# Five layer openings taken as a pair of weight pieces, rounded tokens first, and finer waits for attention outputs

## The chip, the core and the metric

The kernel runs on one core of a Trainium2 chip. The time is what the device needs for one launch, in microseconds (us). The inputs lie in HBM, all work is done by this core's engines: TensorE (PE) multiplies and transposes, its weight loads are listed as PEld; VectorE (DVE), ScalarE (ACT) and GpSimd (POOL) do the rest; SyncE (SP) issues nearly all loads of weights.

## The reference

A stack of layers on 256 tokens of width 1024, float32, cut here to what matters:

```python
# layer 0: sliding-window attention and a state-space mixer; layer 1: stick-breaking attention
hn = rmsnorm(x, norm); mixed = mixer(hn) @ w_out; x = x + mixed
hn = rmsnorm(x, ffn_norm[layer])
x = x + (silu(hn @ w_gate) * (hn @ w_up)) @ w_down          # d_ff 2816
# second block
x = x + mixer(rmsnorm(x, g_mix))    # gated linear attention and block attention, gated by sigmoid(z), then w_out
x = x + memory_attention(rmsnorm(x, g_cross), mem_n)        # w_cq, w_ckv, w_co
x = x + hier_moe(rmsnorm(x, g_moe)) # 32 experts of 512, two for each token
return rmsnorm(x, g_final)
```

## The kernel before

Weights come in **pieces** of 1 MB (128 x 2048 floats), in the order of the table `STREAM`. SP loads piece k into slab k % 6 of a ring once TensorE has freed that slab (`load`, L441, waits for the count `piece_used`). Products keep float32 accuracy by splitting both operands in a rounded part (`hi`) and the rest (`lo`): ScalarE rounds a piece into one of four slabs `piece_hi` (`piece_hi_part`, L765), VectorE subtracts it from the piece, in place (`piece_lo_part`, L1934, count `split`), and TensorE makes three products for each tile (`three_passes`, L1282): hi x hi, hi x lo, lo x hi (the trace shows them as L1285, L1286, L1287).

PSUM has eight banks. Banks 0 to 3 go round for **tiles**: tile n of the list `TILE_PLAN` has bank n % 4, and `open_tile` (L389) waits until tile n - 4 was emptied by VectorE or ScalarE. Banks 4 to 7 hold the 256 x 1024 product that ends a layer: two token blocks (`tb`) by two halves.

A layer opens so. The last output product is done piece by piece (`output_part_split`, L1235); VectorE adds its four banks to the residual X one after the other (`add_residual`, L1869). `output_done` (L1274) waits until the product is finished and frees its last piece. `norm` (L1145) turns X in 16 transposes into four tiles, one for two k-tiles each; the scale by the root is applied later (`keep_roots`, L1840, which reads what `spread_roots`, L1169, puts in bank 4). ScalarE writes the rounded tokens `HT_hi` of each tile (L755, count `ht_hi`), VectorE the rest `HT_lo` (L1922) and so empties the tile. The first piece of the layer (`feature_major_split`, L1296, or `gate_up` in `glu`, L1330) waits before each pair of k-tiles until `HT_lo` of that pair exists:

```python
                            if after and i == first and f == kt % 2 == 0:
                                wait_emptied(pe, after, kt // 2)
                            c = slice(f * P, (f + 1) * P)
                            ins = three_passes(b[:, f * T:(f + 1) * T], (wh[:, kt, c], wl[:, kt, c]),
                                               (hi[:, kt, :], lo[:, kt, :]), kt == 0, kt == KT - 1)
```

A piece of 256 output columns is 2 halves x 8 k-tiles x 3 = 48 products. `glu` does 11 units of a gate piece, an up piece and a down piece. Its unit 0 uses banks 0 and 1; it begins the ffn of both layers (norms 1 and 3). odd_q0 follows norm 2, g_q and g_k norm 4, c_q norm 6.

Attention outputs (two tiles `_o`) are rounded by ScalarE into `MT_hi` (L736) and their rest is taken by VectorE (L1863) before the next product reads them; TensorE waits for both tiles (`wait_all_emptied`, L404). In the mixer of the second block the order on TensorE is: the values of moba (`weighted_values`, L1392), the wait for moba_o, transposes of the gated output (g_oT, L1613), the wait for g_oT, pieces z 6 and z 7, then proj_g and proj_m.

The experts follow the router. Eight teams of four experts use 24 pieces each, without a split. SP may load the first 22 of them early, each when its slab is no longer needed (`put`, L494).

## Time and profile before

| | |
|---|---|
| time, median of 3 runs | 1400.45 us (1399.97 to 1400.62) |
| the profiled execution | 1398.65 us, of which span 1396.5 us |
| busy: TensorE, its weight loads | 1186.7 us (85%), 928.5 us (66%) |
| busy: VectorE, ScalarE, GpSimd | 676.8 us (48%), 469.3 us (34%), 27.0 us (2%) |
| mean granted clock of TensorE | 0.934 |
| read from HBM | 339.80 MB, 245 GB/s over the span |

Span is from the first to the last instruction in the trace; the time has some 2 us around it. In the forty slices of the page TensorE is busy at 0.9 from the fifth slice to the 27th, save one at 0.6 where the small steps of the gated linear attention are, and at 0.5 to 0.7 in the last thirteen. The transfers stand at 0.9 in those, at 0.3 to 0.6 before. An idle time in brackets stands ahead of the instruction whose row it is on, with what ended it.

### The profile page before, as it was taken

To read this page: it belongs to the slowest core of one execution; us is meant where nothing else is said; L and a number is where in the kernel's file an instruction comes from. 1 tells how busy PE (TensorE), PEld (TensorE's weight loads), DVE (VectorE), ACT (ScalarE), POOL (GpSimd) and SP (SyncE) were. 2 spreads that over 40 slices of the span, in tenths; PEclk is the share of its full clock that TensorE was granted. 3 is DMA by queue.
4 is the path that set the end of the run, shared out by engine and by line. 5 is a ranking of instruction groups with operands and counts; after the bars stand their busy time and mean duration, and the time that the engine had idled before them with its cause. 6 is when DMAs were issued, how large, how long until landed. Compare 5 with 4: busy or idle time off the path is not lost.

```text
span 1396.5 us, 19896 instructions
## 1 busy us (share of the span) xinstructions
PE 1186.7 (85%) x8160; PEld 928.5 (66%) x8160; DVE 676.8 (48%) x960; ACT 469.3 (34%) x599; POOL 27.0 (2%) x82
## 2 busy tenths in 40 slices
PE   6999999999999999999998999999674666756665
PEld 5886999998987999998896888884221221212121
DVE  7997475556778575556344857552110110101012
ACT  5555343334665443334344534441010100101001
POOL 2310000000000000000000000000000000000000
PEclk9989999999999999999996999999888988888788
DMA  9523365555434365556452345797999999999995
GB/s 255 120 57 121 107 220 190 189 187 180 144 120 144 112 221 191 188 184 208 139 176 66 121 151 181 314 367 325 421 421 422 422 422 421 422 422 421 423 420 220
DMA packets 137016, 343.41 MB, mean 246 GB/s; under 512 B 9818, under 2 KB 99036, under 8 KB 112372
## 3 DMA queue, kind: packets, MB, share of 16 engines
q1 hardware_dynamic: 135292, 337.96, 64.7%
q0 software_dynamic: 1552, 4.47, 1.8%
q8 instruction: 50, 0.82, 0.2%
q14 instruction: 18, 0.15, 0.0%
q10 hardware_dynamic: 104, 0.02, 0.0%
HBM read 339.80 MB, written 2.62 MB: 245 GB/s over the span
## 4 chain that ended last, share of the span: by engine, by line
PE 60%; DMA 23%; DVE 10%; ACT 3%; issue 3%; SPq 2%; POOL 0%; DVEq 0%; ACTq 0%; POOLq 0%
PE ps L1285 16%; PE ps L1287 15%; PE ps L1286 15%; DMA ring<-in_w_exp_down_dram 11%; DMA ring<-in_w_exp_up_dram 11%; PE ps L1764 4%; PE ps L1739 3%; SPq L526 1%; DVE piece_lo L1939 1%; ACT piece_hi L774 1%; PE ps L1161 1%; DMA MT<-in_ssm_b_im_dram 1%; PE ps L1389 1%; PE ps L1539 1%; PE ps L1685 1%
## 5 line engine op out<-in xcount | busy, mean ns | idle before, releaser
L1285 PE MATMUL ps<-HT_hi,piece_hi 128*128 128x256 f32 x1088 | 311.2, 286 | 7.2 <-DVE HT_lo L1930 4.3
L1286 PE MATMUL ps<-HT_lo,piece_hi 128*128 128x256 f32 x1088 | 308.9, 284 | 0.0
L1287 PE MATMUL ps<-HT_hi,piece_lo 128*128 128x256 f32 x1088 | 308.8, 284 | 0.0
L1939 DVE TENSOR_TENSOR piece_lo<-ring,piece_hi 128x2048 fp32r<-128x2048 f32 x118 | 266.9, 2286 | 83.8 <-ACT piece_hi L774 83.2
L774 ACT ACTIVATE piece_hi<-ring 128x2048 fp32r<-128x2048 f32 x118 | 223.0, 1912 | 196.1 <-PE ps L1287 161.3
L1285 PEld LDWEIGHTS ps<-HT_hi,piece_hi 128*128 128x128 f32 x1088 | 209.8, 193 | 10.8 <-issue 7.8
L1739 PE MATMUL ps<-ring,arena 128*32 128x512 f32 x992 | 139.8, 716 | 87.6 <-DMA ring<-in_w_exp_up_dram 67.6
L1286 PEld LDWEIGHTS ps<-HT_lo,piece_hi 128*128 128x128 f32 x1088 | 209.9, 193 | 0.9
L1287 PEld LDWEIGHTS ps<-HT_hi,piece_lo 128*128 128x128 f32 x1088 | 209.8, 193 | 0.0
L1739 PEld LDWEIGHTS ps<-ring,arena 128*32 128x32 f32 x992 | 38.9, 128 | 182.0 <-issue 181.5
L1764 PE MATMUL ps<-ring,arena 128*32 128x512 f32 x464 | 78.9, 799 | 51.3 <-DMA ring<-in_w_exp_down_dram 51.3
L1764 PEld LDWEIGHTS ps<-ring,arena 128*32 128x32 f32 x464 | 21.2, 140 | 101.1 <-issue 101.1
L2608 DVE COPY arena<-ps 128x512 f32<-128x512 f32 x8 | 5.5, 692 | 143.1 <-PE ps L1764 143.1
L2606 DVE TENSOR_TENSOR arena<-arena,ps 128x512 f32<-128x512 f32 x8 | 5.5, 688 | 137.8 <-PE ps L1739 137.8
L1285 PE MATMUL ps<-piece_hi,HB_hi 128*128 128x512 f32 x176 | 69.7, 396 | 0.0
L1286 PE MATMUL ps<-piece_lo,HB_hi 128*128 128x512 f32 x176 | 69.6, 396 | 0.0
L1287 PE MATMUL ps<-piece_hi,HB_lo 128*128 128x512 f32 x176 | 69.6, 395 | 0.0
L1285 PE MATMUL ps<-piece_hi,HT_hi 128*128 128x256 f32 (+1 forms) x192 | 58.2, 303 | 1.2 <-PE ps L1287 1.2
L1286 PE MATMUL ps<-piece_lo,HT_hi 128*128 128x256 f32 (+1 forms) x192 | 57.7, 300 | 0.0
L1287 PE MATMUL ps<-piece_hi,HT_lo 128*128 128x256 f32 (+1 forms) x192 | 57.7, 300 | 0.0
L1116 ACT ACTIVATE arena<-ps 128x512 f32<-128x512 f32 x8 | 4.8, 597 | 155.8 <-PE ps L1753 155.8
L1960 DVE TENSOR_TENSOR arena<-ps,arena 128x512 f32<-128x512 f32 x22 | 15.2, 692 | 84.3 <-PE ps L1287 84.2
(449 smaller groups left out, 1737.6 us busy)
## 6 DMA issues: line engine op xcount, KB each, us to landing
ring<-in_w_exp_gate_dram SPq DMA_DIRECT2D x64, 1024.0 KB, 18.6
ring<-in_w_exp_up_dram SPq DMA_DIRECT2D x60, 1024.0 KB, 17.6
ring<-in_w_exp_down_dram SPq DMA_DIRECT2D x58, 1024.0 KB, 16.4
ring<-in_ffn_w_gate_dram SPq DMA_DIRECT2D x22, 1024.0 KB, 5.7
ring<-in_ffn_w_up_dram SPq DMA_DIRECT2D x22, 1024.0 KB, 5.4
ring<-in_ffn_w_down_dram SPq DMA_DIRECT2D x22, 1024.0 KB, 7.3
ring<-in_w_in_dram SPq DMA_DIRECT2D x20, 1024.0 KB, 5.4
ring<-in_odd_w_in_dram SPq DMA_DIRECT2D x12, 1024.0 KB, 5.2
```

What stands on the lines that cost most here:

```text
L526: sp.dma_start(dst, src).then_inc(expert_loaded[slot], 16)
L774: act.activation(piece_hi[:, h % HI_SLABS, :], ring[:, k % RING, :], ACT.Copy).then_inc(hi_made, 1)
L1161: ins = pe.transpose(banks[kt // 2][:, c:c + P], (X if raw else XN)[:, tb, kt * P:(kt + 1) * P], ident[:, :])
L1285: pe.matmul(out, sh, mh, start=start, stop=False, skip_group_check=True)
L1286: pe.matmul(out, sh, ml, start=False, stop=False, skip_group_check=True)
L1287: return pe.matmul(out, sl, mh, start=False, stop=stop, skip_group_check=True)
L1389: ins = pe.transpose(b[:, c * P:(c + 1) * P], S[:, h, src * P:(src + 1) * P], ident[:, :])
L1539: ins = pe.matmul(b[0:16, 0:T], alr_w[:, kt, :], part[:, kt, :].bitcast(F32), start=(part is HT_hi and kt == 0), stop=(part is HT_lo and k ...
L1739: ins = pe.matmul(ps[own, 2 + up, :], mGT[:, kt, own], w[e][:, k4, :], start=(kt == 0), stop=(kt == KT - 1))
L1764: ins = pe.matmul(ps[own, 4 + c, :], mHT[:, 2 * half + f, own], w[e][:, f, c * 512:(c + 1) * 512], start=(half == f == 0), stop=(half == f ...
L1939: ve.tensor_tensor(piece_lo[k % RING][:, :], ring[:, k % RING, :], piece_hi[:, h % HI_SLABS, :].bitcast(F32), ALU.subtract).then_inc(split, 1)
L1960: ve.tensor_tensor(by_token(G), by_token(gate), roots[1 + 2 * layer][1].unsqueeze(1).to_broadcast([P, 2, T]), ALU.mult).then_inc(gate_scal ...
```

## The change

Four things, all on TensorE's queue, except for the last line of the diff, by which VectorE reads the gate and up of unit 0 from banks 6 and 7.

- At five openings the first two pieces of the layer are taken together (`opening_pair`). Their first halves go to banks 6 and 7, which do not belong to the round of tiles. For each pair of k-tiles TensorE waits for the rounded tokens only, does the eight products with `HT_hi`, then waits for `HT_lo` and does the other four. The second halves follow as before. The first piece is freed after its second half.
- `output_done` moves from ahead of the norm's transposes to behind the first four of them (norms 1, 2, 3, 4 and 7).
- odd_out (its last two pieces) and c_out wait for one tile of the attention output at a time.
- In the mixer the wait for moba_o moves to ahead of proj_m, and z 6 and z 7 to ahead of the wait for g_oT.

```diff
@@ -74,6 +74,9 @@
 SPLIT_NORMS = (1, 2, 3, 4, 5, 6)
+PAIR_BANKS = {("odd_q0", 0): 6, ("odd_q0", 1): 7, ("g_q", 0): 6, ("g_k", 0): 7, ("c_q", 0): 6, ("c_q", 1): 7}
@@ -384,7 +387,7 @@
         def bank(name, i):
-            return ps[:, TILE_NO[(name, i)] % 4, :]
+            return ps[:, PAIR_BANKS.get((name, i), TILE_NO[(name, i)] % 4), :]
@@ -1142,7 +1145,7 @@
-            def norm(n, wait=True):
+            def norm(n, wait=True, closes=None):
@@ -1161,6 +1164,8 @@
                         ins.then_inc(bank_full, 1)
+                        if closes and kt == 1:
+                            output_done(closes)
                 for _ in range(fillers[1]):
@@ -1232,9 +1237,11 @@
-            def output_part_split(name, pieces, first, opening, closing, hi, lo, ready=None):
+            def output_part_split(name, pieces, first, opening, closing, hi, lo, ready=None, tiles=None):
                 for n, i in enumerate(pieces, first):
+                    if tiles is not None:
+                        wait_emptied(pe, tiles, n - first)
                     if ready is not None:
@@ -1293,6 +1300,39 @@
+            def opening_pair(n, outs, parts):
+                c = slice(0, P)
+                for i in range(4):
+                    pe.wait_ge(ht_hi, 4 * SPLIT_NORMS.index(n) + i + 1)
+                    for kt in (2 * i, 2 * i + 1):
+                        for out, (wh, wl) in zip(outs, parts):
+                            pe.matmul(out[:, 0:T], wh[:, kt, c], HT_hi[:, kt, :], start=kt == 0, stop=False,
+                                      skip_group_check=True)
+                            pe.matmul(out[:, 0:T], wl[:, kt, c], HT_hi[:, kt, :], start=False, stop=False,
+                                      skip_group_check=True)
+                    wait_emptied(pe, f"norm{n}", i)
+                    for kt in (2 * i, 2 * i + 1):
+                        for out, (wh, wl) in zip(outs, parts):
+                            pe.matmul(out[:, 0:T], wh[:, kt, c], HT_lo[:, kt, :], start=False, stop=kt == KT - 1,
+                                      skip_group_check=True)
+            def feature_major_pair(n, tiles):
+                parts = [split_piece(FIRST_PIECE[name] + i, KT) for name, i in tiles]
+                outs = [bank(name, i) for name, i in tiles]
+                opening_pair(n, outs, parts)
+                c = slice(P, 2 * P)
+                for j, (out, (wh, wl)) in enumerate(zip(outs, parts)):
+                    for kt in range(KT):
+                        ins = three_passes(out[:, T:2 * T], (wh[:, kt, c], wl[:, kt, c]),
+                                           (HT_hi[:, kt, :], HT_lo[:, kt, :]), kt == 0, kt == KT - 1)
+                        if j == 1 and kt == 0:
+                            ins.then_inc(piece_used, 1)
+                    ins.then_inc(bank_full, 1)
+                pe.wait_ge(bank_full, full_count(*tiles[1]))
+                pe.nop().then_inc(piece_used, 1)
             def feature_major_split(name, count, hi=HT_hi, lo=HT_lo, first=0, after=None):
@@ -1330,15 +1370,23 @@
-                def gate_up(buf, n, it=None, wait=None, after=None):
+                def first_gate_up():
+                    parts = [split_piece(FIRST_PIECE[name] + j, KT) for j in range(2)]
+                    opening_pair(1 + 2 * layer, [ps[:, 6 + j, :] for j in range(2)], parts)
+                    c = slice(P, 2 * P)
+                    for j, (hi, lo) in enumerate(parts):
+                        for kt in range(KT):
+                            ins = three_passes(ps[:, 6 + j, T:2 * T], (hi[:, kt, c], lo[:, kt, c]),
+                                               (HT_hi[:, kt, :], HT_lo[:, kt, :]), kt == 0, kt == KT - 1)
+                        ins.then_inc(gu_full if j else piece_used, 1)
+                def gate_up(buf, n, it=None, wait=None):
                     if wait is not None:
...
                             for kt in range(KT):
-                                if after and j == f == kt % 2 == 0:
-                                    wait_emptied(pe, after, kt // 2)
                                 c = slice(f * P, (f + 1) * P)
@@ -1359,7 +1407,7 @@
-                gate_up(0, 0, after=f"norm{1 + 2 * layer}")
+                first_gate_up()
                 spread_roots(1 + 2 * layer)
@@ -1370,8 +1418,6 @@
                 down((count - 1) % 2, 3 * count - 1, base + count, stop=True)
-                pe.wait_ge(mix_full, 4 * (RESIDUAL_NO[name] + 1))
-                pe.nop().then_inc(piece_used, 1)
@@ -1498,11 +1544,10 @@
             output_part_split("even_out_a", range(2), 0, 2, 1, MT_hi, even_lo_of)
-            output_done("even_out")
-            norm(1, wait=False)
+            norm(1, wait=False, closes="even_out")
             glu(0)
-            norm(2, wait=False)
-            feature_major_split("odd_q0", 2, after="norm2")
+            norm(2, wait=False, closes="ffn0")
+            feature_major_pair(2, (("odd_q0", 0), ("odd_q0", 1)))
             spread_roots(2)
@@ -1522,15 +1567,14 @@
                 weighted_values(name, A1, lambda h, kb: ov[:, kb, 512 * half + 64 * h:512 * half + 64 * h + 64])
-                wait_all_emptied(pe, name + "_o")
-            output_part_split("odd_out", range(2, 4), 2, 0, 3, MT_hi, odd_lo_of)
-            output_done("odd_out")
-            norm(3, wait=False)
+                if half == 0:
+                    wait_all_emptied(pe, name + "_o")
+            output_part_split("odd_out", range(2, 4), 2, 0, 3, MT_hi, odd_lo_of, tiles="sb1_o")
+            norm(3, wait=False, closes="odd_out")
             glu(1)
-            norm(4, wait=False)
-            feature_major_split("g_q", 1, after="norm4")
+            norm(4, wait=False, closes="ffn1")
+            feature_major_pair(4, (("g_q", 0), ("g_k", 0)))
             spread_roots(4)
-            feature_major_split("g_k", 1)
             token_major_split("g_v", 2)
@@ -1604,7 +1648,6 @@
             weighted_values("moba", PT2, lambda h, kb: m_v[:, kb, 64 * h:64 * h + 64])
-            wait_all_emptied(pe, "moba_o")
             pe.wait_ge(gla_out, 1)
@@ -1613,16 +1656,17 @@
                 ins.then_inc(bank_full, 1)
+            feature_major_split("z", 2, first=6)
             wait_all_emptied(pe, "g_oT")
-            feature_major_split("z", 2, first=6)
             projection_split("proj_g", MT_hi[:, 0:4, :], mixer_lo[:, 0:4, :])
+            wait_all_emptied(pe, "moba_o")
             projection_split("proj_m", MT_hi[:, 4:8, :], mixer_lo[:, 4:8, :])
...
             norm(6, wait=False)
-            feature_major_split("c_q", 2, after="norm6")
+            feature_major_pair(6, (("c_q", 0), ("c_q", 1)))
             for name in ("mem_k", "c_q"):
@@ -1650,10 +1694,8 @@
                 ins.then_inc(bank_full, 1)
-            wait_all_emptied(pe, "c_o")
-            output_part_split("c_out", range(2), 0, 0, 1, MT_hi, lambda kt: c_lo[:, kt, :])
-            output_done("c_out")
-            norm(7, wait=False)
+            output_part_split("c_out", range(2), 0, 0, 1, MT_hi, lambda kt: c_lo[:, kt, :], tiles="c_o")
+            norm(7, wait=False, closes="c_out")
             logits = [open_tile(pe, "router", tb)[:, 0:36] for tb in range(2)]
@@ -1954,7 +1996,8 @@
                     E, G, H = GE[:, buf, :], GH[:, buf, :], HB[:, buf, :]
-                    gate, up = ps[:, 2 * buf, :], ps[:, 2 * buf + 1, :]
+                    first_bank = 6 if u == 0 else 2 * buf
+                    gate, up = ps[:, first_bank, :], ps[:, first_bank + 1, :]
                     by_token = lambda v: v.rearrange("p (f t) -> p f t", t=T)
...
```

TensorE's queue, with the semaphores that a row waits for, at the opening of the first ffn: before, behind the last transposes (L1161).

```order
L1161 MATMUL ps<-ident,X 128x128 [waits residual_ready]
L1161 MATMUL ps<-ident,X 128x128 x5
L1285 MATMUL ps<-HT_hi,piece_hi 128x256 [waits vector_emptied,piece_split]
L1286 MATMUL ps<-HT_lo,piece_hi 128x256
L1287 MATMUL ps<-HT_hi,piece_lo_54 128x256
L1285 MATMUL ps<-HT_hi,piece_hi 128x256
L1286 MATMUL ps<-HT_lo,piece_hi 128x256
L1287 MATMUL ps<-HT_hi,piece_lo_54 128x256
L1285 MATMUL ps<-HT_hi,piece_hi 128x256 [waits vector_emptied]
L1286 MATMUL ps<-HT_lo,piece_hi 128x256
```

And with the change (the transposes are L1164; `piece_lo4_54` and `piece_lo5_55` are the fine parts of the two pieces):

```order
L1164 MATMUL ps<-ident,X 128x128 [waits residual_ready]
L1164 MATMUL ps<-ident,X 128x128 x5
L1310 MATMUL ps<-HT_hi_56,piece_hi_49 128x256 [waits tokens_hi_made,piece_split]
L1312 MATMUL ps<-HT_hi_56,piece_lo4_54 128x256
L1310 MATMUL ps<-HT_hi_56,piece_hi_49 128x256
L1312 MATMUL ps<-HT_hi_56,piece_lo5_55 128x256
L1310 MATMUL ps<-HT_hi_56,piece_hi_49 128x256
L1312 MATMUL ps<-HT_hi_56,piece_lo4_54 128x256
L1310 MATMUL ps<-HT_hi_56,piece_hi_49 128x256
L1312 MATMUL ps<-HT_hi_56,piece_lo5_55 128x256
L1317 MATMUL ps<-HT_lo_57,piece_hi_49 128x256 [waits vector_emptied]
L1317 MATMUL ps<-HT_lo_57,piece_hi_49 128x256 x3
```

The products with `HT_lo` stand behind all eight with `HT_hi`; the first row waits for the rounded tokens instead of the emptied tile.

The mixer, between the values of moba (L1400, L1401) and piece z 6 (L1285), before. Which count of `vector_emptied` a row waits for is not printed: for the first transpose it is the second tile of moba_o, for z 6 the second of g_oT.

```order
L1400 MATMUL ps<-arena 64x256 [waits scalar_emptied]
L1401 MATMUL ps<-arena 64x128
L1613 MATMUL ps<-ident,arena 128x128 [waits gla_out_ready,vector_emptied]
L1613 MATMUL ps<-ident,arena 128x128 x3
L1613 MATMUL ps<-ident,arena 128x128 [waits scalar_emptied]
L1613 MATMUL ps<-ident,arena 128x128 x3
L1285 MATMUL ps<-HT_hi,piece_hi 128x256 [waits piece_split,vector_emptied]
```

And with the change:

```order
L1446 MATMUL ps<-arena 64x256 [waits scalar_emptied]
L1447 MATMUL ps<-arena 64x128
L1656 MATMUL ps<-ident,arena 128x128 [waits vector_emptied,gla_out_ready]
L1656 MATMUL ps<-ident,arena 128x128 x3
L1656 MATMUL ps<-ident,arena 128x128 [waits scalar_emptied]
L1656 MATMUL ps<-ident,arena 128x128 x3
L1292 MATMUL ps<-HT_hi,piece_hi 128x256 [waits vector_emptied,piece_split]
L1293 MATMUL ps<-HT_lo,piece_hi 128x256
```

The rows are in the same order here; the first transpose now waits for a tile of probabilities (moba_pt) only, and z 6 (L1292) for the first tile of moba_o. The two pieces of z stand ahead of the wait for g_oT.

## Rows read from the trace of the kernel before

**Rows 1.** The page: the chain of work that ended last, shares of the span by engine.
```profile
PE 60%; DMA 23%; DVE 10%; ACT 3%; issue 3%; SPq 2%; POOL 0%; DVEq 0%; ACTq 0%; POOLq 0%
```

**Rows 2.** Waits of TensorE, summed: engine, line, waited for: us, times, longest.
```profile
PE ps L1739 <- DMA ring<-in_w_exp_up_dram: 67.6, 14, 6.3
PE ps L1285 <- DVE HT_lo L1930: 4.3, 5, 1.4
```

**Rows 3.** Busy time (PE, PEld, DVE, ACT, POOL) in a stretch, clock, DMA share, GB/s.
```profile
945.00:950.00 5.00, 4.15 (x38) 3.17 (x41) 2.08 (x9) 1.14 (x4) 0.00 (x0) 1.00 0.22 90
```

**Rows 4.** Timeline of TensorE at norm 1 and ffn0: start, us, instruction, idle before and releaser.
```profile
139.11 1.94 PE L1161 MATMUL ps<-ident,X 128*128 128x128 f32 x16 [0.41 <-DVE X L1879]
141.77 0.36 PE L1285 MATMUL ps<-HT_hi,piece_hi 128*128 128x256 f32 x1 [0.73 <-DVE HT_lo L1930]
...
144.85 0.28 PE L1285 MATMUL ps<-HT_hi,piece_hi 128*128 128x256 f32 x1
...
147.73 0.28 PE L1285 MATMUL ps<-HT_hi,piece_hi 128*128 128x256 f32 x1
```

**Rows 5.** Timeline of VectorE, then of ScalarE, there.
```profile
137.18 2.47 DVE L1879 TENSOR_TENSOR X<-X,ps 128x512 f32<-128x512 f32 x4
140.75 3.23 DVE L1930 SCALAR_TENSOR_TENSOR HT_lo<-ps,cols,HT_hi 128x256 fp32r<-128x256 f32 x8 [1.10 <-PE ps L1161]
...
139.77 3.03 ACT L761 ACTIVATE HT_hi<-ps,cols 128x256 fp32r<-128x256 f32 x8 [4.84 <-PE ps L1161]
...
155.86 1.90 ACT L774 ACTIVATE piece_hi<-ring 128x2048 fp32r<-128x2048 f32 x1
```

**Rows 6.** Timeline of VectorE, then of TensorE, behind norm 4.
```profile
655.42 0.42 DVE L1843 COPY arena<-ps 128x256 f32<-128x256 f32 x1
...
656.48 2.28 DVE L1939 TENSOR_TENSOR piece_lo<-ring,piece_hi 128x2048 fp32r<-128x2048 f32 x1
...
660.57 0.36 PE L1285 MATMUL ps<-piece_hi,HT_hi 128*128 128x256 f32 x1 [0.30 <-PE ps L1287]
```

**Rows 7.** Timeline of ScalarE, then of TensorE, at norm 6 and c_q.
```profile
884.65 3.03 ACT L761 ACTIVATE HT_hi<-ps,cols 128x256 fp32r<-128x256 f32 x8 [1.57 <-PE ps L1161]
...
886.62 0.36 PE L1285 MATMUL ps<-HT_hi,piece_hi 128*128 128x256 f32 x1 [1.36 <-DVE HT_lo L1930]
```

**Rows 8.** Around c_out: VectorE; TensorE; the stretch 920 to 925 us.
```profile
919.88 0.69 DVE L1867 TENSOR_TENSOR c_lo<-ps,MT_hi 128x512 fp32r<-128x512 f32 x1 [2.73 <-ACT MT_hi L739]
...
921.85 0.47 PE L1285 MATMUL ps<-piece_hi,MT_hi 128*128 128x512 f32 x1 [1.53 <-DVE c_lo L1867]
...
933.59 1.94 PE L1161 MATMUL ps<-ident,X 128*128 128x128 f32 x16 [0.41 <-PE ps L1287]
...
920.00:925.00 5.00, 3.47 (x16) 2.62 (x15) 3.46 (x3) 0.60 (x1) 0.85 (x4) 1.00 1.02 429
```

**Rows 9.** Timeline of VectorE, then of TensorE, at odd_out.
```profile
438.86 0.69 DVE L1867 TENSOR_TENSOR odd_lo<-ps,MT_hi 128x512 fp32r<-128x512 f32 x1 [1.98 <-ACT MT_hi L739]
...
440.95 0.47 PE L1285 MATMUL ps<-piece_hi,MT_hi 128*128 128x512 f32 x1 [1.53 <-DVE odd_lo L1867]
```

**Rows 10.** The mixer: VectorE; TensorE; the stretch 807 to 809 us.
```profile
802.59 1.31 DVE L1867 TENSOR_TENSOR mixer_lo<-ps,MT_hi 128x512 fp32r<-128x512 f32 x2 [0.45 <-ACT MT_hi L739]
...
798.14 1.53 PE L1389 MATMUL ps<-ident,arena 128*128 128x128 f32 x12 [1.64 <-DVE arena L1859]
...
804.00 1.06 PE L1613 MATMUL ps<-ident,arena 128*128 128x128 f32 x8 [1.53 <-DVE mixer_lo L1867]
806.75 0.55 PE L1285 MATMUL ps<-HT_hi,piece_hi 128*128 128x256 f32 x1 [1.69 <-DVE mixer_lo L1867]
...
812.44 0.41 PE L1287 MATMUL ps<-HT_hi,piece_lo 128*128 128x256 f32 x1
...
807.00:809.00 2.00, 2.00 (x10) 2.00 (x11) 2.00 (x2) 0.55 (x1) 0.00 (x0) 0.50 0.74 279
```

**Rows 11.** Timeline of TensorE: first product with expert weights.
```profile
948.92 3.64 PE L1739 MATMUL ps<-ring,arena 128*32 128x512 f32 x32 [0.61 <-ACT arena L1101]
```

## The prediction

> **What bounds the kernel now.** I read the profile from its end. The chain of work that ended last [rows 1] gives TensorE 60% and the transfers 23%: the program has two halves. The waits of TensorE, summed [rows 2], show the second half: in the experts it waits 67.6 us for up weights, so there the weight stream sets the pace. The same view shows the first half: apart from the experts, the largest sum is 4.3 us for the fine parts of the tokens (HT_lo), in five waits. TensorE is otherwise fed without a break, one 256-column product each 0.12 us. So in the first half only a wait of TensorE is time, and each of them is short.
>
> Whether time saved there reaches the end is answered by the busy time by stretch [rows 3]. Between 945 and 950 us the transfers are at 0.22 of full, moving 90 GB/s: the first team's slabs are loaded, and the rest of the stream waits until TensorE has used one. The stream starts from a signal of TensorE, and then runs without a gap, so a microsecond saved before it is a microsecond at the end.
>
> **Openings of a layer.** TensorE turns the tokens (16 transposes, from 139.11 us), then waits 0.73 us until the fine part of the first two k-tiles exists, and starts at 141.77 [rows 4]. The second half of that first piece starts at 144.85, so 24 products took 3.08 us where 24 x 0.12 is 2.88: 0.20 us more of small waits. ScalarE rounds from 139.77, eight in 3.03 us, VectorE takes the fine part from 140.75, eight in 3.23 us [rows 5]: a pair of k-tiles each 0.81 us, where TensorE eats one in 0.72. The rounded first pair is there at about 139.77 + 0.8 = 140.6, before the transposes end (about 141.04). The change begins with eight products on rounded tokens (0.96 us), then four on the fine ones (0.48 us): fine pair 0 is needed at 142.0 and there at 141.6, and a pair now lasts 1.44 us against 0.81. Both the wait and the small ones go: 0.73 + 0.20. Four openings are like this (odd_q0, the second ffn and g_q are the others): the five waits of [rows 2] are 4.3 us together, and the longest, of c_q, is 1.4, which leaves 0.73 for each. 4 x 0.93 = **3.7 us**.
>
> At 647 us g_q and g_k become a pair, and one drain between a group's last product and the next step goes, the 0.30 us at 660.57 [rows 6]: **0.3 us**. What is new there: the roots are spread after both pieces, 48 products or 5.8 us later. VectorE took them at 655.42 (after other work, so this is the latest date), and the fine part of g_v 1 (2.28 us) queues behind them and one tile of g_q. With the 0.9 won it takes the roots by 655.4 + 5.8 - 0.9 = 660.3 and ends with g_v 1 by 660.3 + 0.4 + 0.7 + 2.3 = 663.7. TensorE began g_v 0 at 660.57, now at 659.3, and wants g_v 1 5.8 us later, at 665.1. Covered by 1.4 us.
>
> At c_q the wait is longer, 1.36 us: ScalarE starts at 884.65, TensorE at 886.62 [rows 7]. With the change TensorE starts on the first rounded pair, at about 884.65 + 0.8 and some 0.15 for the signal, 885.6: 1.0 us, and 0.20 of small waits as above: **1.2 us**.
>
> The first piece of each pair frees its slot 24 products (2.9 us) later. Behind that: SP's next load into that slot, and ScalarE's rounding into that slab. ScalarE comes to the next slab only at 155.86 [rows 5], while the slot is now free at about 141.04 + 72 x 0.12 = 149.7, where it was free at 147.7. Cost 0. Were the cover gone, it would be up to 2 us at each of five places.
>
> **Own-product waits.** The wait for the last output product moves behind the first four transposes. The first row of [rows 4] has 0.41 us of idle there. But those of the second token block wait for VectorE's third addition, which ends about 139.05 (first addition 137.18, four in 2.47 us, [rows 5]). So at norm 1 only two transposes go ahead, 0.2 us; at norms 2 to 4 VectorE ends later and nothing is won; at norm 7 (933.59, [rows 8]) the additions keep up, and most of the 0.41 goes: 0.4. Together **0.6 us**.
>
> **Attention outputs.** At odd_out TensorE waits 1.53 us for both fine tiles and starts at 440.95; the first tile's part starts at 438.86 and takes 0.69 [rows 9]. It may now start at about 439.65: **1.3 us**. The second is needed a piece (24 x 0.23 = 5.6 us) later. At c_out the start is 921.85, the first tile's part is done at 919.88 + 0.69 [rows 8]: start 920.67, **1.2 us**.
>
> **The mixer.** Now: transposes of g_oT at 804.00 after 1.53 us of waiting for the fine parts of moba_o, then z 6 at 806.75 after 1.69 us more [rows 10]. With the change the transposes follow the values at about 804.00 - 1.53 = 802.5, take 8 x 0.12 us, and z 6 needs only tile moba_o 0, whose part starts at 802.59 and is done 0.65 us later. Start at about 803.4: **3.3 us**. Two pieces (11.5 us) then cover both conversions. Their weights were split before that in the kernel before, by queues that do not move.
>
> **The clock.** [...] The single gap of 1.53 us at c_out stands in a stretch with the clock at 1.00 (920 to 925, [rows 8]), so I take the low stretch as gone: **2.5 us**. The bounds are 0 and 2.5.
>
> **Sum.** 3.7 + 0.3 + 1.2 + 0.6 + 1.3 + 1.2 + 3.3 = 11.6, with the clock 14.1 us. The profiled execution took 1398.65 us, so it becomes 1384.6; the median of the runs is 1.8 us above it, 1400.45 - 14.1 = **1386 us**. A difference of 0.2% (2.8 us) is about what a measurement of this kernel tells from none.
>
> **The price that no row has** is that consecutive products now alternate between banks 6 and 7, 48 in each opening, 240 in all. Nearest row: the up piece, in the next bank, starts at 147.73 [rows 4], which is 144.85 + 24 x 0.12: the change of bank costs nothing. I take 0. The other end is the start-up of a stream: the product after 141.77 comes 0.20 us later, 0.08 more; 240 x 0.08 = 19 us. The lower end is 0 too, since the work on the array is the same.
>
> [...]
>
> **Rivals.**
> 1. *The gaps go, the low clock at 806 us stays* (or comes at another place; the stretch of small products before it is not changed, and the first gap of 1.64 us remains). Then 11.6 us: 1389. Chance 0.25.
> 2. *Part of it is taken over by other waits*: late slots, or the roots behind both pieces of g. Half of the gain: about 1394. For it: the rounding chain ScalarE, VectorE, TensorE is a queue of few slabs; against it: the slacks above. Chance 0.08.
> 3. *The stream hides it.* The 22 early pieces must be loaded between 883 and 945 us, and that window gets shorter by 1.2 + 1.2 + 0.4 = 2.8 us. If the stream were full throughout, nothing would be won: 1400. Against it: the share of 0.22 at 945 to 950 [rows 3], nearly 4 us of pause in these 5. Chance 0.03.
> 4. *Slower: alternating banks.* If each of the 240 products lost more than (11.6 + 2.8) / 240 = 0.060 us, the kernel would be slower by over 0.2%. [...] Chance 0.04. [...]
>
> **Chances.** Forecast 0.60; rivals 0.25, 0.08, 0.03, 0.04. Faster by over 0.2%: 0.93; within: 0.03; slower: 0.04. The range reaches from 1382, one more saving of the clock's size (other stretches of small products may keep the full clock too) and 0.2 us more at each of nine waits, to 1393, which takes in rival 1 and most of rival 2. That holds 0.9; the runs of one kernel differ by 0.6 us.
>
> **What would show it.** Waits for HT_lo: none left (one for HTm_lo, 1.4, stays). First product of an opening at once after the transposes. The products of an opening 0.12 us apart: if 0.2, rival 4. One wait of about 0.6 us or less at c_out and odd_out. z 6 about 1 us after the last of the moba values, and the clock at 1.00 there; if it is at 0.50, rival 1. The stretch from the first expert product (now at 948.92, [rows 11]) to the end of the span unchanged at 1396.5 - 948.9 = 447.6 us: if it is longer by what the first half won, rival 3. The forecast is wrong if TensorE shows a new wait for piece_lo in the 30 us behind an opening, or if the first expert product moves by less than 9 us.

## The result, and the profile after

The median of 4 runs is 1383.57 us (1383.30 to 1384.25), beside 1400.21 us of before (4 runs, 1397.86 to 1400.62): ratio 0.9885, 95% interval 0.9868 to 0.9902. Beside another set of runs of before it was 1384.96 against 1399.55, ratio 0.9895 (0.9877 to 0.9913). So the change brings 14.6 to 16.6 us; the two profiled executions are 14.9 us apart (1398.65 and 1383.76), their spans 15.0.

The waits of TensorE, summed, are the answer to [rows 2]:

```profile
PE ps L1781 <- DMA ring<-in_w_exp_up_dram: 64.4, 14, 6.3
...
PE ps L1292 <- DVE HTm_lo L1972: 1.4, 1, 1.4
PE ps L1164 <- DVE X L1919: 1.1, 2, 0.6
```

No row for HT_lo is left. The 1.4 us for HTm_lo (mem_k, which the change left alone) stays. The last row, waits of the transposes for the additions to the residual (X) at norms 2 and 4, stood in the kernel before too, and was shorter:

```profile
PE ps L1161 <- DVE X L1877: 0.8, 2, 0.4
```

So at these norms the moved `output_done` only let TensorE come to the same wait a little earlier.

TensorE at norm 1 and the first opening, to be laid beside [rows 4] (start, us, instruction, idle before):

```profile
138.29 0.40 PE L1294 MATMUL ps<-even_hi,even_lo 128*128 128x512 f32 x1
138.53 2.17 PE L1164 MATMUL ps<-ident,X 128*128 128x128 f32 x16
140.46 0.36 PE L1310 MATMUL ps<-HT_hi,piece_hi 128*128 128x256 f32 x1
140.66 0.28 PE L1312 MATMUL ps<-HT_hi,piece_lo 128*128 128x256 f32 x1
140.78 0.28 PE L1310 MATMUL ps<-HT_hi,piece_hi 128*128 128x256 f32 x1
140.89 0.28 PE L1312 MATMUL ps<-HT_hi,piece_lo 128*128 128x256 f32 x1
```

The opening starts while the last transpose still drains (138.53 + 2.17 = 140.70, the product is at 140.46). From the second product on all 96 of the two pieces start 0.12 us apart. The loop gives each bank two products with rounded tokens before it turns to the other, and one at a time with fine ones: L1310, L1312, L1310, L1312 are bank 6, 6, 7, 7. ScalarE's rounding began at 139.43 here, 0.34 earlier than in [rows 5], of which 0.15 is the earlier start of this execution (first row of the table below).

The two attention outputs and c_q, beside [rows 7, 8, 9]:

```profile
437.12 0.50 PE L1292 MATMUL ps<-piece_hi,MT_hi 128*128 128x512 f32 x1 [0.19 <-DVE odd_lo L1909]
...
873.47 0.35 PE L1310 MATMUL ps<-HT_hi,piece_hi 128*128 128x256 f32 x1 [0.36 <-ACT HT_hi L764]
...
907.10 0.50 PE L1292 MATMUL ps<-piece_hi,MT_hi 128*128 128x512 f32 x1 [0.31 <-DVE c_lo L1909]
```

And the mixer, beside [rows 10]:

```profile
791.44 1.53 PE L1435 MATMUL ps<-ident,arena 128*128 128x128 f32 x12 [1.65 <-DVE arena L1901]
...
795.33 0.44 PE L1447 MATMUL ps<-arena 128*64 128x128 f32 x4
795.70 1.09 PE L1656 MATMUL ps<-ident,arena 128*128 128x128 f32 x8
796.72 0.35 PE L1292 MATMUL ps<-HT_hi,piece_hi 128*128 128x256 f32 x1
...
808.86 0.36 PE L1292 MATMUL ps<-MT_hi,piece_hi 128*128 128x256 f32 x1 [0.41 <-PE ps L1294]
...
800.00:802.00 2.00, 2.00 (x19) 2.00 (x18) 2.00 (x2) 0.00 (x0) 0.00 (x0) 1.00 0.91 373
```

Behind the gap of 1.65 us there is no other, z 6 follows the transposes at once, and the clock in it is 1.00.

**Where the time came from.** The table compares the start of the same instruction of VectorE or ScalarE in two traces. Each kernel has one trace. Of each difference to the changed kernel I took off the difference at the first addition to the residual (137 us), since up to there all kernels of this text are the same. The first column and the row "changed, start" are times in the trace, all others are microseconds later than the changed kernel:

| kernel | start of that addition | rounding at norm 2 | additions ahead of norm 3 | rounding at norm 4 | first mixer_lo | additions of mix_out | rounding at norm 6 | first c_lo | additions of c_out | router |
|---|---|---|---|---|---|---|---|---|---|---|
| changed, start | 137.03 | 330.52 | 447.19 | 640.68 | 795.88 | 853.91 | 872.48 | 906.36 | 914.35 | 925.37 |
| before | 137.18 | 1.29 | 3.66 | 4.75 | 6.56 | 12.35 | 12.02 | 13.37 | 14.55 | 15.03 |
| undo_mixer | 138.61 | 0.01 | -0.02 | -0.02 | -0.05 | 5.42 | 5.43 | 5.42 | 5.42 | 6.98 |
| z_early_only | 139.10 | 0.01 | -0.08 | -0.08 | -0.12 | 1.42 | 1.43 | 1.43 | 1.42 | 2.49 |
| o_late_only | 137.27 | 0.00 | 0.00 | 0.00 | 0.22 | 1.90 | 1.91 | 1.91 | 1.91 | 2.79 |
| undo_closes | 139.44 | 0.14 | 0.08 | 0.08 | 0.20 | 0.42 | 0.09 | 0.13 | 0.12 | 0.13 |
| undo_pairs | 138.35 | 1.10 | 2.13 | 3.23 | 3.76 | 4.00 | 4.01 | 5.35 | 5.35 | 6.29 |
| undo_tiles | 138.48 | 0.00 | 1.23 | 1.23 | 1.33 | 1.57 | 1.57 | 1.56 | 2.74 | 3.47 |
| less_change | 138.75 | 0.00 | -0.06 | -0.06 | -0.01 | -0.01 | 0.00 | -0.01 | -0.02 | -0.02 |
| more_change | 137.20 | 0.00 | 0.07 | 0.07 | 0.37 | 0.64 | 0.64 | 0.28 | 0.28 | 1.47 |
| after_again | 137.11 | 0.01 | -0.08 | -0.08 | -0.07 | 0.16 | -0.18 | -0.14 | -0.14 | -0.14 |
| later_waits | 137.17 | 0.01 | -0.38 | -0.38 | -0.20 | -0.20 | -1.25 | -1.26 | -1.25 | 0.30 |
| fillers | 137.20 | 0.01 | -0.06 | -0.07 | -5.72 | -5.49 | -5.83 | -5.83 | -5.84 | -5.13 |
| all_together | 138.15 | 0.00 | -0.42 | -0.40 | -8.69 | -8.45 | -9.50 | -9.50 | -9.50 | -9.40 |

The row "before" is where the 15 us came from: 12.02 - 6.56 = 5.46 of it in the mixer. The last 0.5 us, between the additions of c_out and the router, are the clock's. The 32 products of the router took 4.20 us before and 3.73 with the change, since the clock fell while they ran before (0.75 on average from 938 to 940 us) and only behind them with the change (0.56 from 925 to 927 us):

```profile
935.91 4.20 PE L1662 MATMUL ps<-router_w,HT 128*128 128x36 f32 x32 [0.39 <-issue]
...
921.20 3.73 PE L1704 MATMUL ps<-router_w,HT 128*128 128x36 f32 x32 [0.99 <-ACT HT L729]
```

The first row is of before, the second of the changed kernel. (The additions of mix_out start some tenths early or late without anything behind them moving: the column beside them doesn't show it.) The first expert product came at 933.74, so from there to the end of the span it is 1381.5 - 933.7 = 447.8 us, where it was 447.6: the experts gave and took nothing.

### The profile page after: what moved, and what is told of

Its sections match the earlier page's. It is cut to its first block, busy times and chain, and to the rows that moved or that the text cites. A ratio compares the mean times of both kernels' runs of the same rounds, so it can differ in the third digit from the quotient of the medians.

```text
span 1381.5 us, 19894 instructions
## 1 busy us (share of the span) xinstructions
PE 1188.3 (86%) x8160; PEld 927.3 (67%) x8160; DVE 675.8 (49%) x960; ACT 469.1 (34%) x599; POOL 26.9 (2%) x82
## 4 chain that ended last, share of the span: by engine, by line
PE 59%; DMA 23%; DVE 11%; ACT 2%; issue 2%; SPq 2%; POOL 0%; DVEq 0%; ACTq 0%; POOLq 0%
PE ps L1292 14%; PE ps L1294 14%; PE ps L1293 14%; DMA ring<-in_w_exp_down_dram 11%; DMA ring<-in_w_exp_up_dram 11%; PE ps L1781 4%; PE ps L1806 3%; DVE piece_lo L1981 2%; SPq L529 1%; PE ps L1310 1%; PE ps L1164 1%; PE ps L1317 1%; PE ps L1312 1%; DMA MT<-in_ssm_b_im_dram 1%; PE ps L1446 1%
## 5 line engine op out<-in xcount | busy, mean ns | idle before, releaser
L1292 PE MATMUL ps<-HT_hi,piece_hi 128*128 128x256 f32 x1008 | 285.9, 284 | 1.2 <-PE ps L1294 1.2
L1294 PE MATMUL ps<-HT_hi,piece_lo 128*128 128x256 f32 x1008 | 285.1, 283 | 0.0
L1293 PE MATMUL ps<-HT_lo,piece_hi 128*128 128x256 f32 x1008 | 285.0, 283 | 0.0
L1781 PE MATMUL ps<-ring,arena 128*32 128x512 f32 x992 | 146.2, 744 | 85.5 <-DMA ring<-in_w_exp_up_dram 64.4
L1292 PEld LDWEIGHTS ps<-HT_hi,piece_hi 128*128 128x128 f32 x1008 | 193.3, 192 | 3.4 <-issue 2.5
L1293 PEld LDWEIGHTS ps<-HT_lo,piece_hi 128*128 128x128 f32 x1008 | 193.3, 192 | 0.9
L1294 PEld LDWEIGHTS ps<-HT_hi,piece_lo 128*128 128x128 f32 x1008 | 193.2, 192 | 0.0
L1806 PE MATMUL ps<-ring,arena 128*32 128x512 f32 x464 | 79.2, 793 | 46.9 <-DMA ring<-in_w_exp_down_dram 46.9
L1292 PE MATMUL ps<-piece_hi,HB_hi 128*128 128x512 f32 x176 | 69.7, 396 | 0.0
L1292 PE MATMUL ps<-piece_hi,HT_hi 128*128 128x256 f32 (+1 forms) x192 | 58.2, 303 | 0.9 <-PE ps L1294 0.6
```

The source lines that it names most:

```text
L1292: pe.matmul(out, sh, mh, start=start, stop=False, skip_group_check=True)
L1293: pe.matmul(out, sh, ml, start=False, stop=False, skip_group_check=True)
L1294: return pe.matmul(out, sl, mh, start=False, stop=stop, skip_group_check=True)
L1781: ins = pe.matmul(ps[own, 2 + up, :], mGT[:, kt, own], w[e][:, k4, :], start=(kt == 0), stop=(kt == KT - 1))
L1806: ins = pe.matmul(ps[own, 4 + c, :], mHT[:, 2 * half + f, own], w[e][:, f, c * 512:(c + 1) * 512], start=(half == f == 0), stop=(half == f ...
```

## The experiments

Each is the changed kernel with one part undone, varied or extended. Times are medians of 4 or 5 runs; the changed kernel's own are 1383.6 and 1385.0. The runs of one kernel lie 1 to 5 us apart, so the size of a part is read from the table.

**The mixer undone.** `undo_mixer`:

```
             ins.then_inc(bank_full, 1)
-            feature_major_split("z", 2, first=6)
             wait_all_emptied(pe, "g_oT")
+            feature_major_split("z", 2, first=6)
             projection_split("proj_g", MT_hi[:, 0:4, :], mixer_lo[:, 0:4, :])
-            wait_all_emptied(pe, "moba_o")
```

with the wait for moba_o ahead of the wait for `gla_out`.

> The changed kernel with the mixer's order as before (wait for moba_o ahead of the transposes of g_oT, z 6 and z 7 behind the wait for g_oT). [...] Rival (the clock came back for another reason, since every stage starts some us earlier): 3.3 us slower, clock 1.00 at z 6.

The forecast's terms for this part are 3.3 us for the two waits and 2.5 for the clock, 5.8 together. Measured 1391.94 us (1389.03 to 1392.21). By the table it is 5.43 + 0.05 = 5.48 us in the mixer, and the rows of [rows 10] are back:

```profile
798.82 1.06 PE L1657 MATMUL ps<-ident,arena 128*128 128x128 f32 x8 [1.53 <-DVE mixer_lo L1909]
801.58 0.55 PE L1292 MATMUL ps<-HT_hi,piece_hi 128*128 128x256 f32 x1 [1.69 <-DVE mixer_lo L1909]
...
802.00:804.00 2.00, 2.00 (x11) 2.00 (x11) 2.00 (x2) 0.37 (x1) 0.00 (x0) 0.50 0.72 293
```

11 products in 2 us instead of 19, at a granted clock of 0.50 instead of 1.00. The waits are 3.22 us, the clock 2.26. The rest of the 8 us is not the mixer's: this execution lost 1.58 ahead of 137 us and 1.56 at the router, where its 32 products took 5.29 us, at a mean clock of 0.68, instead of 3.73 at 1.00.

**One wait of the two.** `z_early_only` puts back the wait ahead of the transposes alone, `o_late_only` the place of z 6 and z 7 alone.

> The changed kernel with the wait for moba_o back ahead of the transposes of g_oT; z 6 and z 7 stay ahead of the wait for g_oT. One gap of about 1.6 us comes back, the other does not. If the low clock at z 6 comes from either gap, or from work up to the values: 1.6 + 2.5 = 4.1 us slower than the changed kernel, granted clock low in the first products of z 6. If it takes both gaps: 1.6 us slower, clock 1.00.

> The changed kernel with z 6 and z 7 back behind the wait for g_oT; the wait for moba_o stays late. One gap of about 1.7 us comes back, behind the transposes. If the low clock comes from this gap (the one just ahead of z 6): 1.7 + 2.5 = 4.2 us slower than the changed kernel, low clock in z 6. If it takes both gaps: 1.7 us slower, clock 1.00.

Measured 1386.90 us (1385.63 to 1388.66) and 1387.06 us (1387.04 to 1391.01). In the mixer they lose 1.43 + 0.12 = 1.55 us and 1.91 - 0.22 = 1.69 us, no more than their gaps of 1.53 and 1.70. `z_early_only`:

```profile
799.24 1.06 PE L1657 MATMUL ps<-ident,arena 128*128 128x128 f32 x8 [1.53 <-DVE mixer_lo L1909]
...
802.00:804.00 2.00, 2.00 (x19) 2.00 (x19) 2.00 (x1) 0.80 (x1) 0.00 (x0) 1.00 1.00 266
```

`o_late_only`:

```profile
798.95 0.36 PE L1292 MATMUL ps<-HT_hi,piece_hi 128*128 128x256 f32 x1 [1.70 <-DVE mixer_lo L1909]
...
802.00:804.00 2.00, 2.00 (x19) 2.00 (x18) 1.25 (x1) 0.00 (x0) 0.00 (x0) 1.00 0.10 41
```

Behind either gap alone the clock stays at 1.00 (one trace each); it fell, to 0.50, only with both behind the gap at the probabilities (1.64 and 1.65 us), in both traces that have all three (before and `undo_mixer`). So the parts of the mixer don't add up: 1.55 + 1.69 = 3.24, together 5.48.

**The pairs undone.** `undo_pairs`: the old loops at the five openings, `PAIR_BANKS = {}`.

> The changed kernel with all five openings as before, one piece after the other, the fine tokens from the second product on. Theory of the forecast: 3.7 + 0.3 + 1.2 = 5.2 us slower than the changed kernel, 0.93 at each of four openings, waits for HT_lo of 0.7 us back at norms 1 to 4 and of 1.4 at norm 6. Rival (the extra 0.3 us that each of the layers won over the forecast belong to the openings): 6.5 us slower, 1.2 to 1.3 at each.

Measured 1389.49 us (1389.01 to 1391.84). By the table 1.10, 1.03 and 1.10 us at norms 1 to 3 and 1.34 at c_q. At norm 4 it is 0.53 up to the mixer, but that mixes two things. The first transposes of the linear attention came at 744.07 us, 737.97 in the changed kernel, so with 1.32 of start off it is 4.78 there, 1.55 more than at norm 4. Behind it 1.0 came back; the stretch at the low clock (0.50) was shorter there (from 743 to 767 us, in the changed kernel from 737.5 to 765). Why it was shorter is not shown. The pairs are worth 1.10 + 1.03 + 1.10 + 1.55 + 1.34 = 6.1 us, and the waits for HT_lo are back, 4.3 us in five.

The same place in this kernel tells why 0.73 us of wait is worth 1.10:

```profile
139.84 2.19 PE L1164 MATMUL ps<-ident,X 128*128 128x128 f32 x16
142.76 0.36 PE L1292 MATMUL ps<-HT_hi,piece_hi 128*128 128x256 f32 x1 [0.73 <-DVE HT_lo L1975]
```

From transposes to product it is 2.92 us, 1.93 in the changed kernel: 0.99. The idle time is counted from the modelled end of the last transpose (139.84 + 2.19 = 142.03), but where nothing is waited for the next product starts 0.24 us before that end. The other 0.1 are the small waits inside the opening: its first 24 products take 3.07 us here and 2.96 in the changed kernel. It is not so everywhere: in the mixer above a gap of 1.53 us cost 1.55 and one of 1.70 cost 1.69.

**The waits for the last output product.** `undo_closes`, at norms 1, 2, 3, 4 and 7:

```
-            norm(1, wait=False, closes="even_out")
+            output_done("even_out")
+            norm(1, wait=False)
```

> The changed kernel with the wait for the last output product back ahead of the transposes, at norms 1, 2, 3, 4 and 7. Theory of the forecast: 0.2 + 0 + 0 + 0 + 0.4 = 0.6 us slower than the changed kernel, and nothing at norms 2 to 4, where VectorE's additions end later anyway. Rival (a removed wait gives back more than its idle time, since the drain of the last product and the start-up of the next lie in it too): about 0.5 us at each of five places, 2.5 us slower.

Measured 1382.97 us (1382.38 to 1387.47): no difference. By the table 0.14 at norm 1 and nothing after. The transposes do start later, yet the opening doesn't. At norm 7, where the forecast had 0.4, the last three additions stand 1.39 us apart in both kernels (in the changed one at 915.74, 917.12 and 918.50, with the last output product at 918.07), and the fourth ends at 919.19. The router needs it: ScalarE sums the squares of the second token block only then, and writes its tiles of the transposed tokens behind that. The first product of the router starts 2.70 us after the start of the fourth addition in both kernels, though the transposes moved:

```profile
918.30 1.91 PE L1164 MATMUL ps<-ident,X 128*128 128x128 f32 x16
918.50 0.69 DVE L1921 TENSOR_TENSOR X<-X,ps 128x512 f32<-128x512 f32 x1 [0.69 <-PE ps L1294]
919.23 1.06 ACT L721 ACTIVATE XN<-X 128x1024 f32<-128x1024 f32 x1 [1.62 <-DVE X L1921]
```

and in `undo_closes`:

```profile
921.04 0.69 DVE L1926 TENSOR_TENSOR X<-X,ps 128x512 f32<-128x512 f32 x1 [0.69 <-PE ps L1294]
921.42 1.94 PE L1164 MATMUL ps<-ident,X 128*128 128x128 f32 x16 [0.41 <-PE ps L1294]
...
923.74 3.73 PE L1709 MATMUL ps<-router_w,HT 128*128 128x36 f32 x32 [0.39 <-issue]
```

**The finer waits.** `undo_tiles`: `tiles=` gone, both tiles waited for.

> The changed kernel with the waits for both tiles of sb1_o and of c_o ahead of the output product. Theory of the forecast: 1.3 us at odd_out and 1.2 at c_out, 2.5 us slower than the changed kernel. Rival: at c_out a part is lost again at the router, which waits for ScalarE, so 1.3 + 0.9 = 2.2 us or less.

Measured 1388.45 us (1387.92 to 1388.97). The table has 1.23 at odd_out and 1.18 at c_out, with both waits at 1.5 again. Another 0.73 us lies at the router, whose products took 4.46 us at a mean clock of 0.82 instead of 3.73 at 1.00, with the low clock (0.50 from 929 us) reaching into them; that the wait at c_out brings this is not shown, since seven kernels that leave c_out alone lose 0.7 to 1.6 us there too.

**The price of a bank.** `less_change` takes one piece, then the other, in both loops of an opening's groups; the first of them:

```
-                    for kt in (2 * i, 2 * i + 1):
-                        for out, (wh, wl) in zip(outs, parts):
+                    for out, (wh, wl) in zip(outs, parts):
+                        for kt in (2 * i, 2 * i + 1):
```

`more_change` leaves this as it is, and takes the second halves product by product in turn from the two banks, so that the first piece is freed with the second.

> The changed kernel with the opening's products in another order: four (two) products of the first piece, then four (two) of the second, so that the bank changes 15 times in an opening's 48 products, not 47. Theory (the change of bank costs nothing): same time as the changed kernel within 0.5 us, products 0.12 us apart. Rival 4 of the forecast, if it cost anything: faster by up to 5 x 32 times the price, 13 us at 0.08 us.

> The changed kernel with the second halves of each pair also product by product between banks 6 and 7, so that 480 products alternate instead of 240. Theory (the change of bank costs nothing): same time within 0.5 us, products 0.12 us apart; the first piece's slot comes free 2.9 us later still, which the queue of slabs has room for. Rival (a price at each change): 240 times the price slower, 19 us at 0.08 us; or, if later slots matter, a wait for the weights' fine part behind each opening.

Measured 1385.16 us (1382.99 to 1386.18) and 1384.21 us (1383.51 to 1385.31). The expectation of `less_change` counts 47 changes of bank in an opening's 48 products, and the prediction takes all 240 products to alternate, but by the loops the changed kernel has 31 changes in an opening: two products with rounded tokens go to one bank, then two to the other. `less_change` has 15, about half, and `more_change`, whose second halves do change at each product, has over twice as many. Up to norm 4, with three openings behind it, the first is 0.06 us earlier and the second 0.07 later; at the first c_lo, behind all five, it is 0.01 earlier and 0.28 later. If all of the 0.28 were the price of the 240 products in turn, it would be 0.001 us each, and the changed kernel run once more (`after_again`) is 0.14 off there too. In the first opening products are 0.12 us apart in all three. So no price is seen, and rival 4 falls. Nor does the clock fall at the openings: in the changed kernel it is 1.00 in each 2 us of 140 to 150, 330 to 342, 448 to 458, 640 to 652 and 872 to 884 us.

**More of the same, and the clock.** `later_waits` moves the wait for sb0_o down to odd_out's first pieces and opens mem_k as a pair; since c_q's pair uses the same two banks, TensorE then waits until both tiles of mem_k are emptied. `fillers` adds transposes whose result nobody reads:

```
+            for _ in range(26):
+                pe.transpose(ps[:, 4, 0:P], ident[:, :], ident[:, :])
             pe.wait_ge(gla_in, 1)
...
+            for _ in range(16):
+                pe.transpose(ps[:, 4, 0:P], ident[:, :], ident[:, :])
             pe.wait_ge(gla_st, 1)
```

`after_again` is the changed kernel beside them.

> The changed kernel itself, once more, beside the two that follow. All stages 0.12 us apart from its first profile at most, except for the stretches at the lower clock ahead of 137 us and at the router, whose length differed between executions of the same instructions: 1382.5 to 1386 us.

> The changed kernel with the same idea at two places that it left alone: the wait for sb0_o moves from behind the first half's values to ahead of odd_out's first pieces, and the two pieces of mem_k open as a pair (banks 6 and 7, rounded tokens first). Theory (in the first half every wait of TensorE is time): the 1.5 us wait for sb0_o goes, and 1.1 of the 1.4 us at mem_k, as at the other pairs: 2.6 us faster than the changed kernel. Rival: at mem_k nothing is won, since norm 6 waits for VectorE and ScalarE, which do other work meanwhile: 1.5 us.

> The changed kernel with 26 and 16 transposes that nobody reads in the two gaps of TensorE ahead of the linear attention (3.4 us at 734.5 and 2.2 us at 744). Theory (gaps ahead of a stretch of small products bring the low clock, as the two gaps of the mixer did): the low stretch of 28 us from 737 us becomes shorter or goes, and the small products run up to twice as fast: 3 to 8 us faster than the changed kernel. Rival (the small products themselves bring it, gap or no gap): the stretch stays, and the second group costs up to 1.6 us more at the lower clock: 0 to 2 us slower.

Measured 1384.96 us (1382.66 to 1386.33), 1383.90 (1382.03 to 1384.42) and 1379.73 (1376.14 to 1381.38). `later_waits`: mem_k gives its 1.05 us, sb0_o only 0.38. The scores do start 1.6 us earlier there, but ScalarE comes to their exponentials at 406.52 (406.38 with the start off), hardly earlier than at 406.74, because two pieces of weights stand ahead of them on its queue: the wait is taken over. `fillers` won 5.65 us between norm 4 and the mixer. The stretch from 745 to 750 us, first of the changed kernel once more (`after_again`), then with fillers:

```profile
745.00:750.00 5.00, 3.73 (x14) 2.36 (x14) 1.08 (x4) 0.00 (x0) 0.00 (x0) 0.50 0.00 0
```

```profile
745.00:750.00 5.00, 5.00 (x36) 3.08 (x36) 0.00 (x0) 0.68 (x3) 0.00 (x0) 1.00 0.00 0
...
754.06 1.32 PE L1426 MATMUL ps<-arena 64*128 64x256 f32 x3 [2.46 <-DVE arena L1934]
...
755.00:760.00 5.00, 5.00 (x26) 4.65 (x25) 4.68 (x12) 0.00 (x0) 0.00 (x0) 0.50 0.00 0
```

The small products run at a granted clock of 1.00, 36 of them in these 5 us and none a filler. Behind the one gap that was left (2.46 us, in the scores of moba) the clock is 0.50. `all_together` has both kernels' edits and 16 fillers in that gap.

> The changed kernel with the later waits of one run (sb0_o, mem_k), the fillers of another, and 16 more filling transposes between the fourth and the fifth score of moba, where the kernel with fillers has a gap of 2.5 us and then the clock at 0.50 for 8 us. Theory (gaps bring the low clock): no low stretch left between 737 and 765 us, some 2 us faster than with the fillers alone, and 1.4 us (0.4 and 1.05) for the later waits: 1376 us. Rival (products of the scores and their VectorE-bound rate bring the low clock, or it comes later): 1378 to 1380 us.

Measured **1375.63 us** (1374.52 to 1376.00), ratio to before 0.9827 (0.9813 to 0.9840): it beats both kernels, with 1376 expected. The same stretch has no low clock, and neither has any other from norm 4 to the router (1.00 in each 5 us from 640 to 915 us):

```profile
754.68 1.01 PE L1430 MATMUL ps<-arena 64*128 64x256 f32 x3 [0.56 <-DVE arena L1939]
...
755.00:760.00 5.00, 5.00 (x40) 4.70 (x39) 4.97 (x14) 0.00 (x0) 0.00 (x0) 1.00 0.02 3
```

## Why the prediction was right

It said 1386, from 1382 to 1393, and 14.1 us won; it was 1383.6 (a second time 1385.0), 15.0 in the spans. The mechanism was the forecast one: nearly all of the gain came at the waits that were named, and reached the end. Term by term, with the table's figures:

- *Openings*, four at 0.93 and 0.3 for g: 4.0 forecast; 1.10, 1.03, 1.10 and 1.55, so 4.8. Right mechanism, too small: the forecast took the idle time in brackets as the whole price, and left out 0.24 us of overlap that comes back with it. Of its 0.20 us of small waits 0.08 are the start of a stream, which stays (the second product is 0.20 us behind the first in the changed kernel too). Why g gives 0.45 us more than the others, and not 0.3, is open. *c_q*: 1.2 forecast, 1.34 measured. The 0.15 us for the signal in that term is read from no row of the kernel before; from the start of the rounding to the first product it was 0.99 us, with 0.95 forecast.
- *Own-product waits*: 0.6 forecast, 0.1 measured. This step failed. At norm 7 "the additions keep up" overlooked that the router needs the fourth addition too, which waits for the last product in any order. At norm 1 it was 0.14 for the 0.2, at norms 2 to 4 nothing, as said.
- *odd_out and c_out*: 1.3 and 1.2 forecast, 1.23 and 1.18 measured.
- *Mixer*: 3.3 and, for the clock, 2.5; 5.8 together; 5.46 between the kernels, 5.48 by undoing it, of which the clock is 2.26. The 2.5 was the author's estimate, and no run shows it as such; the runs showed the 2.26, with the granted clock at 0.50 and products 0.21 us apart instead of 0.12 (`undo_mixer`, 802 to 804 us). Rival 1 fell: the clock went to 1.00 and the undone mixer brought the low stretch back. The forecast's reason, three gaps close to each other (1.64, 1.53 and 1.69 us, the last two of them taken away by the change), stood the test of putting back one at a time.
- *Alternating banks*: 0 forecast, none seen. The 240 at which the forecast set its rival are 240 products, but 155 changes of bank.
- *Covers*: by its letter one sign of being wrong came true, a wait for piece_lo less than 30 us behind an opening (norm 4's, at g_r). But the same product stood 0.33 us before, put down to the drain, so no time came with it, and rival 2 fell. The first row is of before, the second of the changed kernel:

```profile
672.64 0.36 PE L1285 MATMUL ps<-piece_hi,HT_hi 128*128 128x256 f32 x1 [0.33 <-PE ps L1287]
...
666.11 0.36 PE L1292 MATMUL ps<-piece_hi,HT_hi 128*128 128x256 f32 x1 [0.30 <-DVE piece_lo L1981]
```

- *To the end*: the stretch from the first expert product stayed, 447.8 beside 447.6 us. Rival 3 fell.

Not forecast: 0.5 us at the router, where the low clock came behind its products instead of into them. It is luck: in eight of the twelve runs of the experiments the low stretch reached into them (mean clock 0.68 to 0.82 over the 32 products) and cost 0.7 to 1.6 us. Luck is in the total too. The parts undone one by one add up to 4.8 + 1.3 + 0.1 + 1.2 + 1.2 + 5.5 = 14.1 us, the forecast to a tenth, because the openings gave about 0.9 more (c_q with them) and the own-product waits and the mixer 0.8 less. With the 0.5 at the router that is 14.6 of the 15.0; the other 0.4 are not assigned. And the forecast reckoned that runs of one kernel differ by 0.6 us; they differ by 1 to 5.

## What to carry to other kernels

Where one engine is fed without a break, price a wait by the starts of instructions on both sides of it, not by its idle time alone (0.73 us idle was 0.99 at an opening), and look for the second producer behind the one that the wait names: `output_done` and sb0_o had one, and gave 0.1 and 0.4 us instead of 0.6 and 1.5. Gaps as close to each other as those of the mixer should be counted together: from both waits of the mixer to one of them TensorE won 3.8 to 3.9 us, for a gap of 1.5 or 1.7, since the clock came back with it (from 0.50 to 1.00). To compare variants within a per mille, lay the starts of the same instructions side by side; the medians mix the edit with what happens elsewhere.

## What the runs showed of the hardware

- The clock fell to 0.50 with three gaps of 1.64, 1.53 and 1.69 us within 10.3 us (796.50 to 806.75 in the kernel before), and stayed at 1.00 with two of them, the first and either of the others (`z_early_only`, `o_late_only`). Behind a single gap of 2.46 us in `fillers` it fell to 0.50 too. Filling the gaps of 3.37 and 2.21 us of the changed kernel with transposes whose result nobody reads took the low clock from the small products behind them (0.50 from 737.5 to 750 us in the changed kernel, 1.00 there in `fillers`), so here it was the gaps that brought it, not the size of the products.
- A change of PSUM bank from one product to the next cost nothing that shows: 0.12 us from start to start within one bank (`less_change`, four products at a time), in pairs (the changed kernel), and in turn (`more_change`, second halves).
- The same instructions have low stretches of different length. At 90 to 92 us, where all kernels are the same, the changed kernel and `undo_closes` read

```profile
90.00:92.00 2.00, 1.99 (x18) 1.77 (x19) 1.94 (x5) 1.90 (x5) 0.00 (x0) 1.00 0.03 8
```

```profile
90.00:92.00 2.00, 1.02 (x6) 0.71 (x6) 1.72 (x4) 1.78 (x5) 0.00 (x0) 0.50 0.00 0
...
926.00:928.00 2.00, 2.00 (x21) 2.00 (x21) 0.57 (x3) 2.00 (x2) 0.00 (x0) 1.00 1.03 430
```

  The last two rows are of `undo_closes`. It comes to the first addition 2.41 us later (137.03 and 139.44 in the table). Not all of this is the clock's: 0.92 are there before the low stretch, where TensorE waited longer for VectorE, 0.96 us in the changed kernel and 2.06 in `undo_closes`:

```profile
76.72 0.43 PE L1510 MATMUL ps<-arena 128*128 128x64 f32 x2 [0.96 <-DVEq L2175]
...
77.64 0.43 PE L1510 MATMUL ps<-arena 128*128 128x64 f32 x2 [2.06 <-DVEq L2180]
```

  The router's stretch costs 0 to 1.6 us, the lengthening of its 32 products. Both are of the size of the 1 to 5 us between the runs of one kernel; that they make them is not shown, since each kernel has one trace. What decides their length stays open.
